# A retention / conformer / ConvFFN trunk step on one core: another order of the opening stage, one key split ahead of the gates, one product on VectorE, LayerNorm means in three PSUM banks

## The chip, the cores and the metric

One core of a Trainium2 chip runs the whole program; nothing else runs on the chip. The metric is the device time of one execution in microseconds, as a median over runs. The core has TensorE (PE, with its weight loads PEld), VectorE (DVE), ScalarE (ACT), GpSimd (POOL) and the queue engine SyncE (SP), all synchronised by semaphores written out by hand in the kernel.

## The reference, cut to what matters

One layer (DEPTH = 1) is applied to 1024 latent tokens and, apart from them, to 128 context tokens, all in float32:

```python
mod = silu(cond) @ ada_w + ada_b              # cond = c (latent) or c_ctx (context); 6 x 1024 columns
sh1, sc1, g1, sh2, sc2, g2 = split(mod, 6)
h    = rms_norm(x, n1_pre) * (1 + sc1) + sh1
proj = h @ w_in                               # 8192 columns: q, k, v, g | u_a, u_b | gate_ret, gate_conv
o, s_f, s_b = bidirectional_retention(rope(q), rope(k), v, ...)   # chunks of 128, 4 heads of 256
ret  = (silu(g) * head_group_norm(o)) @ ret_w_out
u    = depthwise_conv31(u_a * sigmoid(u_b))
conv = silu(layer_norm(u, cln_w, cln_b)) @ conv_w_out
x    = x + g1 * rms_norm((sigmoid(gate_ret) * ret + sigmoid(gate_conv) * conv) @ w_mix_out, n1_post)
h2   = rms_norm(x, n2_pre) * (1 + sc2) + sh2
a, b = split(depthwise_conv3(h2 @ ffn_w_up), 2)       # 2 x 2816 columns
x    = x + g2 * rms_norm((silu(a) * b) @ ffn_w_down, n2_post)
```

The outputs are x of both parts and the final states s_f, s_b of the context tokens.

## The kernel before, in words

**Arithmetic.** Every large matmul is made of three with 32-bit reduced operands: each factor is split into a high part (`*_hi`, a rounded copy, mostly on ScalarE) and a low part (`*_lo` = value minus high, on GpSimd or VectorE), and hi x hi, hi x lo and lo x hi are summed in PSUM (line 936 is the helper `mm` for nearly all of them). The 1152 tokens are 9 tiles of 128 (`NT`), or 3 groups of 384 (`NTG`, `TG`); 1024 features are 8 blocks `k` (`KT`). Each engine runs one program in written order; what sets the order is the code alone, and each piece waits for counts of semaphores.

**Opening.** Columns 0 to 2047 of `ada_w` (8 chunks `ada_p` of 1 MB, `ada_early`) are multiplied by silu(cond) as each lands. x comes in three loads (`x_load`, tiles 0-2, 3-5, 6-7, and the context tile). ScalarE squares x (`square`, `root`), VectorE scales it (`normed`). `mod_turns` turns the rows of mod into columns. Then 24 units j = 8 g + k (group g, block k) go through a chain: TensorE turns three tiles of x (`x_turn`, banks 5, 7, 6), ScalarE applies shift and scale (`modulated`, result `hf`), VectorE splits into `A_hi`, `A_lo` (`halves`; for some units, `ON_ACT`, ScalarE writes `A_hi` too). `first_u` multiplies them by the first two 128-column pieces of w_in: per group g the piece e = 0, block by block as the chain delivers, and then e = 1. `first_u` is followed by `q_half(0)`, whose first bank is free when ScalarE has read the result of e = 0 (`sig`, line 1500). The weight pieces come through four raw slots (`chunk_load`, SyncE), `split_w` (ScalarE) and `lo_w` (GpSimd).

**Projections** (96 to 727 us of the profile): TensorE runs without a gap; VectorE does rotary products and the 31-tap convolution, ending with the last channel block.

**Retention** (from 727 us): steps s = -9 to 35. In a step TensorE does, for the key/value chunk `piece(s)`, the outer product `outer_b` (needs `kb_lo` of GpSimd and `vb_lo` of VectorE, each after ScalarE's `key_b`), and between the parts of the recurrence a third of a gate projection (`gate_part(x)`, 24 matmuls, x = 0 to 47). `W_GATE0` gates stand ahead of the steps; the table `gate_of` gives the others to steps. The key/value chunks come back from memory in three slots (`kv_load`).

**Merge.** 16 tiles `n` of three groups (e = 3 n + g). The LayerNorm of the convolution branch runs beside the first tiles: GpSimd sums over blocks (`ln_tree`), TensorE averages over partitions by a matmul with `mean_w` (`ln_mean` after e = 5, 6, 8, `ln_var` after e = 11, 13, 15), VectorE centres (`c_raw`, line 2437).

**ConvFFN.** 22 column pairs j. The first two (`plain`) are multiplied directly, the others by seven products of sums (operands `O_hi`, `O_lo`; units A11, S2, S3, A22, S1, A12, S4), with token sums `T_raw`, `T_hi`, `T_lo` built on VectorE at the beginning. Per j: `centre_tap` (ScalarE, `f_cv`), `side_taps` (VectorE), `silu`, `product` (the SwiGLU product, in place in `f_cv[0]`), and `g_store` to memory, after which `centre_tap(j + 1, 0)` may overwrite `f_cv[0]`:

```python
if j and kind == 0:
    act.wait_ge(q.g_st, 16 * j)
```

## Time and profile before

| | us |
|---|---|
| median of 3 runs (2215.16 to 2217.37) | 2216.73 |
| the profiled execution | 2214.35 |
| its span | 2212.4 |
| TensorE busy | 2147.2 (97%) |
| VectorE busy | 1580.7 (71%) |
| ScalarE busy | 787.5 (36%) |
| GpSimd busy | 975.2 (44%) |

The profile page divides one execution by engine, by time and by group of instructions. TensorE's busy share is high nearly everywhere; of its 40 slices of 55 us only the first (7 tenths) and second (8 tenths with the weight loads) stand out. Therefore the rows that matter are those in which TensorE waits, and those of the engines that end its waits. A matmul's busy time is modelled; its start, and the distance between starts, are measured.

### The profile page before, as it was taken

The numbers are of one execution on the slowest core, as the hardware profiler recorded it, in microseconds if no ns is written. First come the engines' busy times: TensorE is split into PE (matmuls) and PEld (weight loads), VectorE is DVE, ScalarE is ACT, GpSimd is POOL, SyncE is SP. The second block draws the span as 40 slices with busy tenths as digits, with TensorE's granted clock in tenths as the row PEclk, the third lists the DMA queues.
The fourth block names the chain that finished last, engine by engine and source line by source line (L and its number), as shares of the span: only waits on it lengthen the run. The fifth ranks groups of instructions, "written<-read, shape, count | busy, mean of one in ns | idle before, by whom it ended". The sixth has DMA issues, their size and how long they took to land.

```text
span 2212.4 us, 31598 instructions
## 1 busy us (share of the span) xinstructions
PE 2147.2 (97%) x12483; PEld 1968.5 (89%) x12483; DVE 1580.7 (71%) x1789; ACT 787.5 (36%) x1328; POOL 975.2 (44%) x620
## 2 busy tenths in 40 slices
PE   7899999999999899999999999989999999999998
PEld 3788988988988799999889998889999999978887
DVE  3489589589589467676436536689998898766775
ACT  3501201101101266665537333343333333434342
POOL 0313423423323356665372230056665665565654
PEclk9999999999999999999999999999999999999999
DMA  9333342442432445545454444313232322385653
GB/s 304 105 119 102 120 126 92 129 128 86 130 105 87 151 149 169 165 147 156 158 193 156 131 163 137 105 30 84 66 89 61 82 68 74 116 298 172 210 176 130
DMA packets 246578, 291.78 MB, mean 132 GB/s; under 512 B 12225, under 2 KB 198945, under 8 KB 246433
## 3 DMA queue, kind: packets, MB, share of 16 engines
q1 hardware_dynamic: 175553, 219.22, 31.3%
q10 hardware_dynamic: 69472, 65.83, 9.2%
q0 software_dynamic: 1408, 4.72, 0.5%
...
## 4 chain that ended last, share of the span: by engine, by line
PE 88%; DVE 4%; DMA 2%; ACT 2%; POOL 1%; issue 1%; SPq 0%; ACTq 0%; DVEq 0%; POOLq 0%
PE ps L936 87%; DVE f_cv L2550 1%; DMA ada_p<-in_ada_w 1%; POOL f_cv L2099 1%; PE ps L1146 1%; DVE T_raw L2510 1%; PE ps L1194 0%; DMA r_raw<-rT_d 0%; PE ps L987 0%; DMA sh_row<-gain_d 0%; DVE T_lo L2532 0%; DMA g_raw<-g_d 0%; ACT f_cv L1842 0%; PE ps L1281 0%; POOL Wa_lo L1955 0%
## 5 line engine op out<-in xcount | busy, mean ns | idle before, releaser
L2230 DVE SCALAR_TENSOR_TENSOR conv_y<-u_in,VC,conv_y 128x1167 f32<-128x1167 f32 x240 | 396.0, 1650 | 7.4
L1955 POOL TENSOR_TENSOR Wa_lo<-W_raw,Wa_hi 128x1024 fp32r<-128x1024 f32 x58 | 142.7, 2467 | 409.4 <-ACT Wa_hi L1404 409.3
L936 PE MATMUL ps<-A_hi,Wa_hi 128*128 128x384 f32 x768 | 270.8, 353 | 6.2 <-DVE A_lo L2195 5.3
L936 PE MATMUL ps<-A_hi,Wa_lo 128*128 128x384 f32 x768 | 258.9, 337 | 0.0
L936 PE MATMUL ps<-A_lo,Wa_hi 128*128 128x384 f32 x768 | 258.7, 337 | 0.0
L2550 DVE SCALAR_TENSOR_TENSOR f_cv<-f_in,VF,f_cv 128x1023 f32<-128x1023 f32 (+1 forms) x176 | 210.7, 1248 | 11.2 <-ACT f_cv L1842 9.4
L1955 POOL TENSOR_TENSOR D_lo<-F_raw,D_hi 128x1024 fp32r<-128x1024 f32 x66 | 162.4, 2463 | 99.6 <-ACT D_hi L1404 99.6
L2587 DVE TENSOR_TENSOR g_lo<-g_raw,g_hi 128x384 fp32r<-128x384 f32 x66 | 138.6, 2110 | 81.1 <-ACT g_hi L1404 81.1
L2094 POOL TENSOR_TENSOR O_lo<-E,O_hi 128x512 fp32r<-128x512 f32 x80 | 130.4, 1630 | 147.1 <-ACT O_hi L1404 147.1
L936 PE MATMUL ps<-Wb_hi,A_hi 128*128 128x512 f32 x432 | 180.0, 417 | 0.0
L936 PE MATMUL ps<-Wb_hi,A_lo 128*128 128x512 f32 x432 | 170.7, 395 | 0.0
L2094 POOL TENSOR_TENSOR O_lo<-F_raw,O_hi 128x512 fp32r<-128x512 f32 x68 | 111.5, 1642 | 132.2 <-ACT O_hi L1404 132.2
L936 PE MATMUL ps<-Wb_lo,A_hi 128*128 128x512 f32 x432 | 169.3, 392 | 0.0
L936 PE MATMUL ps<-D_hi,g_hi 128*128 128x512 f32 x396 | 155.2, 392 | 4.4 <-POOL D_lo L1955 2.4
L936 PE MATMUL ps<-D_hi,g_lo 128*128 128x512 f32 x396 | 154.6, 390 | 0.0
L936 PE MATMUL ps<-D_lo,g_hi 128*128 128x512 f32 x396 | 154.6, 390 | 0.0
L936 PEld LDWEIGHTS ps<-A_hi,Wa_hi 128*128 128x128 f32 x768 | 145.7, 190 | 9.6 <-DVE A_lo L2195 5.6
L1404 ACT ACTIVATE Wa_hi<-W_raw 128x1024 fp32r<-128x1024 f32 x58 | 60.4, 1056 | 255.7 <-DVE qk_st L2256 211.0
L936 PE MATMUL ps<-B_hi,O_hi 128*128 128x288 f32 x608 | 141.6, 297 | 5.5 <-POOL O_lo L2094 4.9
L936 PEld LDWEIGHTS ps<-A_lo,Wa_hi 128*128 128x128 f32 x768 | 145.7, 190 | 0.8
L936 PEld LDWEIGHTS ps<-A_hi,Wa_lo 128*128 128x128 f32 x768 | 145.0, 189 | 0.0
L936 PE MATMUL ps<-B_hi,O_lo 128*128 128x288 f32 x608 | 141.2, 297 | 0.0
...
## 6 DMA issues: line engine op xcount, KB each, us to landing
...
```

The source lines that it names most:

```text
L936: return pe.matmul(out, l, r, start=start, stop=stop)
L1146: last = pe.transpose(ps[:, 2, x * P:(x + 1) * P], qt[:, n % 5, x // 2, (x % 2) * P:(x % 2 + 1) * P], ident[:, :])
L1404: return act.activation(dst, src, ACT.Copy)
L1955: return pool.tensor_tensor(dst, x, Fv(hi), ALU.subtract)
L2094: pool.tensor_tensor(O_lo[o % 4][:, :, :], op_src(o)[2], Fv(O_hi[o % 4][:, :, :]), ALU.subtract).then_inc(q.w_lo, 1)
L2099: pool.tensor_tensor(f_cv[0][:, :], f_cv[0][:, :], f_cv[1][:, :], ALU.mult).then_inc(q.fprod, 1)
L2230: dve.scalar_tensor_tensor(out=y, in0=x, scalar=tap, in1=y, op0=ALU.mult, op1=ALU.add).then_inc(q.conv_step, 1)
L2510: dve.tensor_tensor(out, x, y, op).then_inc(q.t_ok, 1)
L2550: dve.scalar_tensor_tensor(out=f_cv[kind][:, o[0]:o[1]], in0=f_in[kind][:, x[0]:x[1]], scalar=VF[:, col:col + 1], in1=f_cv[kind][:, o[0]:o ...
L2587: dve.tensor_tensor(g_lo[c % 4][:, :], g_raw[c % 4][:, :], Fv(g_hi[c % 4][:, :]), ALU.subtract).then_inc(q.dg_lo, 1)
```

## The change

The change has five parts.

1. **Transfers of the opening.** The two condition vectors go first on SyncE's queue and have a semaphore of their own (`c_in`); the first transpose waits for them alone. Four semaphores instead of two let chunk n of `ada_w` be issued when chunk n - 4 has landed. The second load of x is issued behind chunk 7, and with the third load and the raw pieces 2 to 5 behind it. The first loads of `ada_w`'s later columns, the rotary tables and the norm weights move from ScalarE's queue to SyncE's.
2. **Order of the opening on the engines.** `x_turn` stands ahead of the block's matmuls and not behind; ScalarE's second squares come behind the first weight split, its third squares after unit 7 (before: after unit 11); VectorE scales the second tiles of x at unit 3 and the third at unit 8 (before: ahead of all units, and at unit 12); `ON_ACT` holds for units 1, 4, 7, 9, 12, 15; weight pieces 1 to 5 are split after units 3, 15, 19, 21, 23.
3. **Retention.** `key_b(0)` on ScalarE and GpSimd and `value_b(0)` on VectorE come ahead of the gates and of VectorE's mod columns; one gate instead of two stands ahead of the steps, and step -9 gets a gate.
4. **LayerNorm.** The three means are written to banks 4, 5, 6 and the three variances to 7, 4, 5, so that `ln_mean(g)` no longer waits for `centre` of g - 1.
5. **ConvFFN.** `product(0)` moves from GpSimd to VectorE, behind `side_taps(0, 1)`.

```diff
-        ada_in = [q.ada_in0, q.ada_in1]
+        ada_in = [q.ada_in0, q.ada_in1, q.ada_in2, q.ada_in3]
...
-        W_GATE0, N_STEP = 2, HEADS * NT
+        W_GATE0, N_STEP = 1, HEADS * NT
         gate_of, n_gate = {}, W_GATE0
-        for s_ in [-8, -7, -6, -5, -4, -2, -1] + list(range(N_STEP)):
+        for s_ in [-9, -8, -7, -6, -5, -4, -2, -1] + list(range(N_STEP)):
...
-        ON_ACT = lambda k: k % 4 == 3
+        ON_ACT = lambda j: j < 2 * KT and j % KT % 3 == 1
...
+        LN_BANK = {("mean", 0): 4, ("mean", 1): 5, ("mean", 2): 6, ("square", 0): 7, ("square", 1): 4, ("square", 2): 5}
...
             def ada_chunk(n):
 
-                if n >= 2:
-                    sp.wait_ge(ada_in[n % 2], 16 * (n // 2))
-                sp.dma_start(ada_p[:, n, :, :], ada[:, :, n * 2 * P:(n + 1) * 2 * P]).then_inc(ada_in[n % 2], 16)
+                if n >= 4:
+                    sp.wait_ge(ada_in[n % 4], 16)
+                sp.dma_start(ada_p[:, n, :, :], ada[:, :, n * 2 * P:(n + 1) * 2 * P]).then_inc(ada_in[n % 4], 16)
...
+            sp.wait_ge(q.hT_lo, N_A)
+            for x in range(2):
+                sp.dma_start(ada_w[:, x, :, :], ada[:, :, (16 + x) * P:(17 + x) * P]).then_inc(ada_in[x], 16)
...
             pe.wait_ge(q.ident_ok, 3)
-            pe.wait_ge(q.tab_in, 80)
+            pe.wait_ge(q.c_in, 32)
...
             for n in range(8):
-                if n == 3:
+                if n == 4:
                     row_turns()
...
                         for k in range(KT):
+                            ahead = KT * g + (k + 4 if e == 0 else 11 + (k // 2 if g else 0))
+                            while turned < min(ahead, N_A):
+                                x_turn(turned)
+                                turned += 1
                             if e == 0:
                                 pe.wait_ge(q.hT_lo, KT * g + k + 1)
                             mm(o, wh[:, k, :], A_hi[:, tiles, k, :], k == 0, False)
                             mm(o, wh[:, k, :], A_lo[:, tiles, k, :], False, False)
                             last = mm(o, wl[:, k, :], A_hi[:, tiles, k, :], False, k == KT - 1)
-                            ahead = KT * g + (k + 4 if e == 0 else 11 + k // 2)
-                            while turned < min(ahead, N_A):
-                                x_turn(turned)
-                                turned += 1
...
             def ln_mean(g):
 
                 pe.wait_ge(q.ln_sum, 3 * LN_SUM_MEAN[g])
-                if g:
-                    pe.wait_ge(q.ln_dve, ln_done["centre", g - 1])
                 tok = slice(g * TG, (g + 1) * TG)
-                mm(ps[:, 6, 0:TG], mean_w[:, :], c_sq[:, 0, tok], True, True).then_inc(q.ln_pe, 1)
+                mm(ps[:, LN_BANK["mean", g], 0:TG], mean_w[:, :], c_sq[:, 0, tok], True, True).then_inc(q.ln_pe, 1)
...
-            for g in range(2):
+            def squares(g):
+
                 for t in range(3 * g, 3 * g + 3):
                     square(t)
                 root(g)
+            squares(0)
             split_w(0)
-            split_w(1)
+            squares(1)
             act.wait_ge(q.mod_ok, 2)
             for j in range(N_A):
                 modulated(j)
-                if j == 11:
-                    for t in range(6, NT):
-                        square(t)
-                    root(2)
-                if j in (15, 19):
-                    split_w((j - 15) // 4 + 2)
+                if j == 7:
+                    squares(2)
+                if j in (3, 15, 19, 21, 23):
+                    split_w((3, 15, 19, 21, 23).index(j) + 1)
...
-            act.wait_ge(q.hT_lo, N_A)
-            ada_load(0)
-            ada_load(1)
-            for r in range(3):
-                rope_load(r)
-            gn_load(0)
-            gn_load(1)
...
+            key_b(0)
             for x in range(W_GATE0):
                 gate_out(x)
                 if x == 0:
                     split_w(N_S1 + 2, (q.q_ps, 72))
-            key_b(0)
...
             for o in range(2 * 4):
                 op_lo(o)
-            product(0)
             for x in (U_A11, U_S2, U_S3, U_A22):
                 op_lo(op_no(2, x))
...
+            meaned(0)
             normed(0)
             row_half(0)
...
             row_half(1)
+            meaned(1)
             dve.wait_ge(q.ada_used, 16)
...
             for j in range(N_A):
-                if j == 12:
+                if j == 3:
+                    normed(1)
+                if j == 8:
+                    meaned(2)
                     normed(2)
                 halves(j)
...
             side_taps(0, 1)
+            dve.wait_ge(q.ftap, max(tap_no(0, 0), tap_no(0, 1)))
+            dve.wait_ge(q.fsilu, 1)
+            dve.tensor_tensor(f_cv[0][:, :], f_cv[0][:, :], f_cv[1][:, :], ALU.mult).then_inc(q.fprod, 1)
             T_lo_part(0)
```

What that makes of the order, at three places. SyncE's queue from the program's start, before (`rows` are the small parameter vectors, `ada_p` the chunks of 1 MB, x3 and x4 are that many transfers):

```order
L643 DMA ada_p<-in_ada_w 128x8x256 x2
L638 DMA x_all<-in_x_sample 128x3x1024
...
L643 DMA ada_p<-in_ada_w 128x8x256 x4
L638 DMA x_all<-in_x_sample 128x3x1024
L643 DMA ada_p<-in_ada_w 128x8x256 x2
L697 DMA W_raw<-in_w_in 128x8x128 x2
L638 DMA x_all<-in_x_sample 128x2x1024
```

and the same queue now:

```order
L650 DMA rows<-in_c 8x128
L650 DMA rows<-in_c_ctx 8x128
L647 DMA ada_p<-in_ada_w 128x8x256 x2
L642 DMA x_all<-in_x_sample 128x3x1024
L647 DMA ada_p<-in_ada_w 128x8x256 x2
...
L647 DMA ada_p<-in_ada_w 128x8x256 x3
L701 DMA W_raw<-in_w_in 128x8x128
L647 DMA ada_p<-in_ada_w 128x8x256
L642 DMA x_all<-in_x_sample 128x3x1024
L701 DMA W_raw<-in_w_in 128x8x128
```

Two more chunks stand ahead of the small vectors (the line of dots), and the second load of x stands behind the last chunk.

ScalarE at the beginning of retention, before (from the last mod columns; `gate_sg` is a gate's read-out, `kb_hi` and `vb_hi` the key and value split, `st_b` the state's output):

```order
L1404 ACTIVATE mod<-ps 128x16
L1404 ACTIVATE gate_sg<-ps 128x384
L1577 DMA gate_d<-gate_sg 128x384
L1404 ACTIVATE Wa_hi<-W_raw 128x1024
L1404 ACTIVATE gate_sg<-ps 128x384
L1577 DMA gate_d<-gate_sg 128x384
L1404 ACTIVATE kb_hi<-kv 128x256
L1587 ACTIVATE vb_hi<-kv,dkt 128x256
L1404 ACTIVATE st_b<-ps 128x512
```

and now:

```order
L1419 ACTIVATE mod<-ps 128x16
L1419 ACTIVATE kb_hi<-kv 128x256
L1592 ACTIVATE vb_hi<-kv,dkt 128x256
L1419 ACTIVATE gate_sg<-ps 128x384
L1582 DMA gate_d<-gate_sg 128x384
L1419 ACTIVATE Wa_hi<-W_raw 128x1024
L1419 ACTIVATE st_b<-ps 128x512
L1663 DMA out<-st_b 128x2x256
L1419 ACTIVATE kb_hi<-kv 128x256
L1592 ACTIVATE vb_hi<-kv,dkt 128x256
L1419 ACTIVATE gate_sg<-ps 128x384
```

The first split moved ahead of both read-outs, and the second split stands ahead of the second read-out.

GpSimd in the same place, before and then now (`conv_d` is the store of the last convolution block, two transfers):

```order
L1997 TENSOR_TENSOR vg_st<-vg_st,gn_head 128x256 x9
L1955 TENSOR_TENSOR Wa_lo<-W_raw,Wa_hi 128x1024
L1976 DMA conv_d<-conv_y 128x1024
L1976 DMA conv_d<-conv_y 128x128
L1955 TENSOR_TENSOR kb_lo<-kv,kb_hi 128x256 x3
```

```order
L2002 TENSOR_TENSOR vg_st<-vg_st,gn_head 128x256 x9
L1960 TENSOR_TENSOR kb_lo<-kv,kb_hi 128x256
L1960 TENSOR_TENSOR Wa_lo<-W_raw,Wa_hi 128x1024
L1981 DMA conv_d<-conv_y 128x1024
L1981 DMA conv_d<-conv_y 128x128
L1960 TENSOR_TENSOR kb_lo<-kv,kb_hi 128x256 x2
```

Only the first `kb_lo` moved; the weight split and the store are still ahead of the second.

## Rows read from the trace of the kernel before

**Rows 1.** waits of TensorE, whole program: us in total, times, longest

```profile
PE ps L936 <- POOL O_lo L2094: 4.9, 2, 4.4
...
PE ps L936 <- DVE c_raw L2437: 4.1, 1, 4.1
```

**Rows 2.** timeline of TensorE, opening: start, us, line, what, count [idle before]

```profile
10.88 0.25 PE L952 MATMUL ps<-ident,rows 16*128 16x16 f32 x1 [10.88 <-DMA dec<-in_ret_decay_bwd]
...
11.65 13.34 PE L936 MATMUL ps<-ada_p,cs 128*2 128x256 f32 x48 [0.52 <-ACT cs L1421]
...
42.55 3.61 PE L936 MATMUL ps<-ada_p,cs 128*2 128x256 f32 x16
...
70.23 0.45 PE L936 MATMUL ps<-A_hi,Wa_hi 128*128 128x384 f32 x1 [2.56 <-DVE A_lo L2195]
...
95.72 0.80 PE L936 MATMUL ps<-Wa_hi,A_hi 128*128 128x512 f32 x1 [5.30 <-ACT sig L1500]
```

**Rows 3.** timeline of SyncE's queue, opening

```profile
9.36 15.16 SPq L643 DMA_DIRECT2D ada_p<-in_ada_w  x4
```

**Rows 4.** tile ada_p, from issue to landing

```profile
DMA to landing us min/median/max: 5.3/10.1/13.2
```

**Rows 5.** stretch 30 to 40 us: its us, engines busy, TensorE's clock, DMA, GB/s

```profile
30.00:40.00 10.00, 8.44 (x41) 3.15 (x39) 2.83 (x6) 3.43 (x7) 0.00 (x0) 1.00 1.08 357
```

**Rows 6.** timeline of ScalarE, opening

```profile
34.00 1.06 ACT L1438 ACTIVATE sq_t<-x_all 128x1024 f32<-128x1024 f32 x1 [7.08 <-DMA x_all<-in_x_sample]
...
48.60 1.79 ACT L1455 ACTIVATE hf<-ps,mod,hscale 128x384 f32<-128x384 f32 x3 [3.33 <-DVE hscale L2208]
```

**Rows 7.** timeline of VectorE, opening

```profile
50.95 0.56 DVE L2195 TENSOR_TENSOR A_lo<-hf,A_hi 128x384 fp32r<-128x384 f32 x1
...
67.05 2.08 DVE L2181 TENSOR_SCALAR x_all<-x_all,rst 128x1024 f32<-128x1024 f32 x3
...
75.00 1.47 DVE L2195 TENSOR_TENSOR A_lo<-hf,A_hi 128x384 fp32r<-128x384 f32 x1
```

**Rows 8.** timeline of GpSimd, opening

```profile
73.66 2.40 POOL L1955 TENSOR_TENSOR Wa_lo<-W_raw,Wa_hi 128x1024 fp32r<-128x1024 f32 x1 [25.41 <-ACT Wa_hi L1404]
```

**Rows 9.** timeline of TensorE, start of retention

```profile
738.67 0.35 PE L936 MATMUL ps<-vb_hi,kb_hi 128*128 128x256 f32 x1 [2.60 <-DVE vb_lo L2286]
...
742.42 0.55 PE L936 MATMUL ps<-vb_hi,kb_hi 128*128 128x256 f32 x1 [2.80 <-DVE vb_lo L2286]
...
755.40 0.38 PE L936 MATMUL ps<-vb_hi,kb_hi 128*128 128x256 f32 x1 [0.49 <-POOL kb_lo L1955]
```

**Rows 10.** timeline of SyncE's queue, start of retention

```profile
742.96 3.07 SPq L719 DMA_DIRECT2D kv<-qkvg_d  x3
```

**Rows 11.** tile kv, 720 to 745 us, from issue to landing

```profile
DMA to landing us min/median/max: 8.5/8.6/8.7
```

**Rows 12.** stretches in which TensorE's granted clock was 0.5

```profile
92.50:99.30 6.80, 3.58 (x9) 2.92 (x10) 0.00 (x0) 6.05 (x6) 6.80 (x3) 0.50 0.53 169
...
1133.60:1136.90 3.30, 3.14 (x8) 2.56 (x9) 0.02 (x1) 2.76 (x1) 0.95 (x2) 0.50 0.02 5
...
1474.90:1478.20 3.30, 3.30 (x16) 3.30 (x15) 0.25 (x1) 1.63 (x2) 0.00 (x0) 0.50 1.07 273
```

**Rows 13.** timeline of GpSimd, start of ConvFFN

```profile
1461.22 11.60 POOL L2099 TENSOR_TENSOR f_cv<-f_cv,f_cv 128x1152 f32<-128x1152 f32 x1 [12.13 <-DVE f_cv L2550]
```

**Rows 14.** timeline of ScalarE, start of ConvFFN

```profile
1476.57 1.35 ACT L1842 ACTIVATE f_cv<-f_in,VF 128x1152 f32<-128x1152 f32 x1 [16.17 <-DMA g_d<-f_cv]
```

**Rows 15.** timeline of VectorE, start of ConvFFN

```profile
1439.36 1.36 DVE L2510 TENSOR_TENSOR T_raw<-T_raw,T_raw 128x1152 f32<-128x1152 f32 x1
...
1467.81 2.55 DVE L2510 TENSOR_TENSOR T_raw<-T_raw,B_lo 128x2304 f32<-128x2304 f32 x1
...
1477.95 4.01 DVE L2550 SCALAR_TENSOR_TENSOR f_cv<-f_in,VF,f_cv 128x1023 f32<-128x1023 f32 x4 [7.60 <-ACT f_cv L1842]
...
1494.53 2.47 DVE L2583 TENSOR_TENSOR f_in<-ps,f_in 128x576 f32<-128x576 f32 x3
```

More of the change, by code:

```diff
@@ L495, in s_no @@
             return 4 * (j - PLAIN) + which
-        wl_base = [sum(32 if m < N_S1 and m % 6 >= 2 else 16 for m in range(N_L) if chunk_sem(m) == x) for x in range(4)]
+        wm_base = [sum(32 if m < N_S1 and m % 6 >= 2 else 16 for m in range(N_L) if chunk_sem(m) == x) for x in range(4)]
+        wl_base = [wm_base[x] + (16 * M_CHUNKS // 3 if x < 3 else 0) for x in range(4)]
         tile_base = [16 * len(range(x, HEADS * NT, 5)) for x in range(5)]
@@ L639, in ada_chunk @@
             def ada_chunk(n):
-                if n >= 2:
-                    sp.wait_ge(ada_in[n % 2], 16 * (n // 2))
-                sp.dma_start(ada_p[:, n, :, :], ada[:, :, n * 2 * P:(n + 1) * 2 * P]).then_inc(ada_in[n % 2], 16)
+                if n >= 4:
+                    sp.wait_ge(ada_in[n % 4], 16)
+                sp.dma_start(ada_p[:, n, :, :], ada[:, :, n * 2 * P:(n + 1) * 2 * P]).then_inc(ada_in[n % 4], 16)
+            for n, name in enumerate(("c", "c_ctx")):
+                v = a[name] if len(a[name].shape) == 1 else a[name][0]
+                sp.dma_start(rows[n * KT:(n + 1) * KT, 0, :], v.rearrange("(k p) -> k p", p=P)).then_inc(q.c_in, 16)
             ada_chunk(0)
@@ L702, in chunk_load @@
                                      w_in_s[:, 2 * j:2 * j + 2, 2 * g + s, h * 256:(h + 1) * 256]).then_inc(done, 16)
-            for n in range(2):
-                chunk_load(n)
+            for n in range(4, 7):
+                ada_chunk(n)
+            chunk_load(0)
+            ada_chunk(7)
+            x_load(1)
+            chunk_load(1)
             sp.wait_ge(x_in[0], X_IN[0])
@@ L1411, in split_w @@
                 copy(w_hi[chunk_slot(n)], chunk_raw(n)).then_inc(q.w_hi, 1)
-            for n, name in enumerate(("c", "c_ctx")):
-                v = a[name] if len(a[name].shape) == 1 else a[name][0]
-                act.dma_start(rows[n * KT:(n + 1) * KT, 0, :], v.rearrange("(k p) -> k p", p=P)).then_inc(q.tab_in, 16)
             act.dma_start(tab[:, :], a["shape_table"]).then_inc(q.tab_in, 16)
@@ L1451, in modulated @@
                 outs = [t3(hf[:, j % 6, :])]
-                if ON_ACT(k):
+                if ON_ACT(j):
                     outs.append(A_hi[:, 3 * g:3 * g + 3, k, :])
@@ L2192, in halves @@
                 hi, lo = (x[:, 3 * g:3 * g + 3, k, :] for x in (A_hi, A_lo))
-                if not ON_ACT(k):
+                if not ON_ACT(j):
                     then(dve.tensor_copy(hi, h_))
@@ L2265, in _, with value_b @@
                     taps_u(i, range(2 * NT, CW))
+            def value_b(b):
+                dve.wait_ge(q.kb_hi_ok, 2 * b + 2)
+                dve.scalar_tensor_tensor(out=vb_lo[:, :], in0=kv[:, b % 3, 1, :], scalar=dkt[:, b // 8, 3:4], in1=Fv(vb_hi[:, :]),
+                                         op0=ALU.mult, op1=ALU.subtract).then_inc(q.kb_vlo, 1)
+            value_b(0)
             dve.wait_ge(q.adaU_ok, 4)
```

82 lines of the change are left out of this document (42 added, 40 removed).

## The prediction

> **What bounds the kernel now.** I read the page's table of engines and the slices first: TensorE works in 97% of the span, and only the first two of its 40 slices stand out. So I listed TensorE's waits and looked which of them the change touches. Four places came out.
>
> - Opening. TensorE does nothing until 10.88, when the last small table lands; its first transpose waits for all five [rows 2]. Three chunks of `ada_w` then take 13.34 and later ones 3.61 each, so at full clock the three would be 10.8. Chunk 7 ends at 42.55 + 3.61 = 46.16, ScalarE's first `modulated` starts at 48.60 [rows 6], and the chain's 24 units set the time from there: `first_u` ends at 95.72 - 5.30 = 90.42. Behind it stands one wait of 5.30 for `sig`, and from 92.5 to 99.3 the granted clock is 0.50 (1.2 of 2.4 GHz) after that idle time [rows 12].
> - Retention: two waits of 2.60 and 2.80 for `vb_lo`, with matmuls of 0.55 after them where 0.35 is usual [rows 9].
> - LayerNorm: one wait of 4.1 for `c_raw` [rows 1], and a clock of 0.50 from 1133.6 to 1136.9 [rows 12].
> - ConvFFN: a wait of 4.4 for `O_lo` [rows 1] and half clock at 1474.9 to 1478.2 with DMA share 1.07 [rows 12]. Behind it lies a GpSimd product of 11.60 [rows 13], a `centre_tap` that waited 16.17 for the product's store [rows 14], and VectorE, idle 7.60 ahead of the side taps [rows 15].
>
> In the projections, from 95.72 to retention, TensorE runs without a gap, so what the opening gains arrives at the end in full.
>
> **The opening, up to the first unit.** The condition vectors now go first and alone release the transpose. An `ada_p` load needs at least 5.3 from issue to landing [rows 4]; TensorE can start chunk 0 near 8 in place of 11.65. Chunk 0 at half clock is 7.2 and chunk 1 is 3.6, so chunk 2 starts near 19 (before: 25.0 - 3.6 = 21.4). Six chunks are 6 x 3.61 = 21.7, and I allow 1.5 for the two sets of turns between them: chunk 7 ends at 42.2. The distance from there to the first unit was 48.60 - 46.16 = 2.4 and I keep it: first unit at about 45.0, **-3.6**. Supply: eight chunks and the first x are 10.0 MB, at 357 GB/s [rows 5] 28 us after the start, so chunk 7 is there by 34 while TensorE wants it at 38.6. The second x, now behind chunk 7, has 2.1 MB more in front (with the first raw weight): issue by 31, landing by 36 to 41, since each of SyncE's issues can hold the queue (four took 15.16 [rows 3]). Its squares need three times 1.06 [rows 6], to about 44.3. The bounds are 0 (x late, then ScalarE comes late) and -6 (chunk 0 starts at 7 with nothing lost).
>
> **The 24 units.** Before, 48.60 to 90.42: 41.8. Removed is part of the wait of 2.56 at the group's change [rows 2], because the third squares come four units earlier, -1.1; TensorE's transposes stand one block earlier, and `ON_ACT` takes A_hi for different units, -2.4. Added is that five weight splits instead of two run on GpSimd while VectorE splits. One such split is 2.40 on GpSimd [rows 8], and a VectorE instruction beside it took 1.47 instead of 0.56 [rows 7]: 0.9 each for three more, 2.7, of which two thirds lie in VectorE's idle time, +0.9. The scaling of the second x (2.08 for three [rows 7]) stands between units 2 and 3 instead of before them and is hidden by the time in which ScalarE is ahead: 0 to +2. Sum **-2.6**, bounds -6 and +5.
>
> **The hand-over to `q_half(0)`.** The wait of 5.30 arose since splits, twelve loads on ScalarE's own queue and a table load stood between the last unit and `sig`. The loads are gone from there and the weights are split earlier, so `sig` comes with the end of the e = 0 part: **-5.3** (bounds -3 and -5.3), and with no gap the stretch at half clock goes. In its 6.8 us the first 3.6 after 95.72 were work at half speed: **-1.8** (0 to -1.8). `ada_w`'s next load now waits for the last unit; its user stands near 84 and the load needs up to 13.2 [rows 4] in the worst case; I put 0 for it, at most +0.5 of TensorE beside the other q pieces. Opening together: -3.6 - 2.6 - 5.3 - 1.8 = **-13.3**; bounds -6 and -18.
>
> **Retention.** The first key split comes before the gates, so the wait of 2.60 goes. The second does not go whole: on GpSimd the weight split (2.40, by the like in the opening [rows 8]) and the store still stand ahead of `kb_lo(1)`, which leaves about 1.4 of 2.80. Without these waits the steps come earlier, and chunk 3 now meets its own load. It is issued at 742.96 [rows 10] behind a wait for the convolution's store, lands 8.5 later [rows 11] = 751.5, and with the splits the outer product starts at 753.1 at best, against 755.40 before [rows 9]. So at most 2.3 can be gained by then, and about 1.6 comes back as a longer idle time with the clock at half behind it: **-0.7** (bounds +1 and -6; the latter if the load too is issued earlier).
>
> **LayerNorm.** `ln_mean(1)` waited 4.1 for VectorE to have centred group 0, in the same bank. With banks of its own it needs GpSimd's sum alone, which no row shows late. So the 4.1 goes, and half of the 3.3 at half clock: **-5.7** (bounds 0, if GpSimd's sum is late in its place, and -5.8).
>
> **ConvFFN.** A VectorE product of that shape takes 1.36 [rows 15], in place of 11.60. VectorE runs on, without idle time, until 1470.36 (1467.81 + 2.55); with the product ahead of this the side taps of j = 1 can start at 1470.36 + 1.4 = 1471.8, not at 1477.95: 6.1 earlier. The product is done by 1462.6 and its store had time; `centre_tap(1, 0)` needs 1.35 [rows 14] and is done by 1471. The chain onwards (VectorE's sums at 1494.53 [rows 15], which hold TensorE) moves by the same amount, less what TensorE's own work limits. GpSimd, rid of the product, splits `O_lo` when it is due, and the 4.4 and most of the half clock behind it go. VectorE's 1.4 moves `T_lo` later by as much: **-5.5** (bounds -1.6 and -7.6).
>
> The Trainium skill ("SBUF — State Buffer", section "Who interferes with whom") says that VectorE and GpSimd share a port pair that is an exclusive lock: where both instructions need it, and one with two SBUF inputs does, the second to issue waits until the first is done. The product's 11.60 [rows 13] is in keeping with that; the 1.47 against 0.56 [rows 7] beside a split of 2.40 [rows 8] is not the full length of the split. By that rule the ConvFFN term would be at its full bound, and the splits in the opening would be a rival, below.
>
> **The sum.** -13.3 - 0.7 - 5.7 - 5.5 = -25.2; the profiled execution's own 2214.35 gives 2189.2. The median is 2.4 above that execution, so on its scale 2191.6, and I say **2192**.
>
> **The rivals.**
> - *The second x holds ScalarE.* The queue lets x go only once chunk 7 is issued; if it lands near 45 and not 41, its squares, which stand ahead of the first unit, end at 48.4, and the first unit starts where it did. For: an issue takes 3.8 us on this queue [rows 3], and DMA is full in that stretch (1.08 [rows 5]). Against: with four semaphores the chunks themselves wait less. -25.2 + 3.6 + 1.4 more for the group phase = -20.2: 2197. Chance 0.20.
> - *GpSimd blocks VectorE for the whole split.* Five splits lie among the units now; if each stops VectorE for 2.4 and not 0.9, that is 5 x 1.5 = 7.5 more: -17.7, 2199. For: 11.60 for one product beside an unbroken VectorE. Against: 1.47 beside 2.40. This is the page's rule of the exclusive lock. Chance 0.10.
> - *Everything counts in full.* The kv load is early, both `vb_lo` waits go with their half clock (-5), ConvFFN at -7.6: -32, 2185. Chance 0.10.
> - *The opening stays at half clock: slower.* TensorE now begins earlier than the data flow, and has a pause before every chunk. If therefore 1.2 GHz is granted through the opening, each of six chunks takes 7.2 instead of 3.6 (+21.6) and the 144 matmuls of `first_u`, 384 columns each, 0.32 instead of 0.16 (+23): together about +45 on a base of -25 + 13 (the opening's other gains become meaningless as TensorE bounds it) gives +10 to +33, middle about 2230. It decides only if over half of 8 to 85 us is at 1.2 GHz. For: 48 matmuls from 11.65 show a slow start, and idle stretches of 4 to 5 us are followed by half clock [rows 12]. Against: 1.00 in 30 to 40 us with TensorE busy 8.44 of 10 [rows 5]. Chance 0.03.
> - The forecast: 0.57.
>
> **How the numbers follow.** The likeliest case alone has 2186 to 2199 (opening -18 to -8, the others' bounds partly cancelling). With the two rivals above it and the one below, 2183 to 2204 leaves out under 2 in 10. A change of under 0.2% (4.4 us) can hardly be told from none; only a loss of most terms brings it there. Faster 0.95, same 0.02, slower 0.03.
>
> **What would show it.** TensorE's first matmul near 5 and chunk 7 ending near 42; the first `modulated` near 45; `q_half(0)`'s start near 83 with no wait for `sig`, and a clock of 1.00 behind it. VectorE's `A_lo` at 1.5 beside each split, not 2.9. In retention no wait of 2.60, and a new one, for the load of the key/value chunk or its splits, at the fourth outer product. No wait for `c_raw`. A product of 1.4 on VectorE, and the side taps of j = 1 about 10 us after it and not 16.8 us after GpSimd's start. I am wrong if `modulated` starts at 48 (first rival), if `A_lo` takes over 2 us (second), or if ln's matmul waits as long for GpSimd as it did for VectorE.

## The result, and the profile after

The changed kernel takes 2197.05 us in the median (2195.45 to 2200.72), before 2217.05; the ratio is 0.9914 (95% interval 0.9899 to 0.9929). That is 20.0 us faster where 25 were forecast (2192), inside the stated range. The profiled execution took 2197.59, its span 2195.8 against 2212.4. So the profiled pair is 16.8 apart and the medians are 20.0 apart: the kernel before was profiled in an execution 2.7 under its median, the changed one 0.5 over.

The sum came nearer than its terms, as the table shows. Its last column comes from laying the two traces over each other, matmul by matmul ("the overlay" from here on): how much earlier each one starts.

| part | forecast | overlay, profiled pair |
|---|---|---|
| opening, read at 100 us and still so at 728 | -13.3 | -4.8 |
| retention, read at 1100 us | -0.7 | -3.7 (-2.6 by 800 us) |
| LayerNorm | -5.7 | -6.0 at 1200 us, of which 1.1 is lost again by 1440 |
| ConvFFN, 1440 to 1600 us | -5.5 | -4.0 |
| sum | -25.2 | -17.4 (last matmul -17.0, spans -16.6) |

The recorded expectations below give other figures for the same four parts: 4.5, 3.8, 5.2 and 3.9. The table's are read at the places that it names.

TensorE's waits over the whole program (us in total, times, longest), for [rows 1]. First one more of the kernel before:

```profile
PE ps L936 <- DVE A_lo L2195: 5.3, 5, 2.6
```

and then those of the changed kernel:

```profile
PE ps L953 <- DVE A_lo L2198: 7.3, 6, 2.6
PE ps L953 <- DMA ada_p<-in_ada_w: 7.0, 2, 6.2
...
PE ps L953 <- POOL kb_lo L1960: 4.9, 3, 2.9
PE ps L953 <- ACT f_in L1419: 4.0, 1, 4.0
PE ps L969 <- DMA rows<-in_c_ctx: 3.9, 1, 3.9
...
PE ps L953 <- POOL O_lo L2099: 0.9, 2, 0.5
```

The waits for `c_raw` and `sig` are gone and the longest for `O_lo` is 0.5, as forecast. But the waits for `A_lo` have risen from 5.3 to 7.3, and in place of the 4.4 for `O_lo` stand 4.0 for `f_in`. TensorE's timeline of the opening and of the first outer products, for [rows 2, 9]:

```profile
3.93 0.26 PE L969 MATMUL ps<-ident,rows 16*128 16x16 f32 x1 [3.93 <-DMA rows<-in_c_ctx]
10.42 8.98 PE L953 MATMUL ps<-ada_p,cs 128*2 128x256 f32 x32 [6.23 <-DMA ada_p<-in_ada_w]
20.20 7.17 PE L953 MATMUL ps<-ada_p,cs 128*2 128x256 f32 x32 [0.80 <-DMA ada_p<-in_ada_w]
...
39.77 3.62 PE L953 MATMUL ps<-ada_p,cs 128*2 128x256 f32 x16
...
54.77 0.44 PE L953 MATMUL ps<-A_hi,Wa_hi 128*128 128x384 f32 x1 [2.63 <-DVE A_lo L2198]
...
86.56 0.69 PE L953 MATMUL ps<-A_hi,Wa_hi 128*128 128x384 f32 x1 [1.96 <-DVE A_lo L2198]
...
92.66 0.39 PE L953 MATMUL ps<-Wa_hi,A_hi 128*128 128x512 f32 x1
...
726.92 0.28 PE L953 MATMUL ps<-vb_hi,kb_hi 128*128 128x256 f32 x1
...
733.49 0.39 PE L953 MATMUL ps<-vb_hi,kb_hi 128*128 128x256 f32 x1 [1.51 <-POOL kb_lo L1960]
...
746.43 0.35 PE L953 MATMUL ps<-vb_hi,kb_hi 128*128 128x256 f32 x1 [2.90 <-POOL kb_lo L1960]
```

TensorE is ready at 4 and then waits 6.2 us for chunk 0. Chunk 7 ends at 43.39 (before 46.16), and ScalarE's first unit starts at 45.81, 2.8 earlier. From there to `q_half(0)` it is 46.9 us. Before, `first_u` ended 41.8 after the first unit; the forecast had 39.2. In retention the wait of 2.60 is gone, the second is 1.51 where about 1.4 was forecast, and the forecast new wait at the fourth outer product is there (2.90).

The first rival asked whether the late second x holds ScalarE:

```profile
41.87 1.06 ACT L1450 ACTIVATE sq_t<-x_all 128x1024 f32<-128x1024 f32 x1 [5.77 <-DMA x_all<-in_x_sample]
```

It landed at 41.9 (forecast 36 to 41, the rival near 45), and its squares end at 45.1, just before the first unit. So it came later than forecast, but it did not put the first unit at 48.

VectorE in the units, for [rows 7]:

```profile
49.48 4.19 DVE L2184 TENSOR_SCALAR x_all<-x_all,rst 128x1024 f32<-128x1024 f32 x3
...
72.14 1.45 DVE L2198 TENSOR_TENSOR A_lo<-hf,A_hi 128x384 fp32r<-128x384 f32 x1
...
75.14 2.71 DVE L2198 TENSOR_TENSOR A_lo<-hf,A_hi 128x384 fp32r<-128x384 f32 x1
...
78.35 2.23 DVE L2198 TENSOR_TENSOR A_lo<-hf,A_hi 128x384 fp32r<-128x384 f32 x1
...
84.24 2.26 DVE L2198 TENSOR_TENSOR A_lo<-hf,A_hi 128x384 fp32r<-128x384 f32 x1
```

and GpSimd beside it, for [rows 8]:

```profile
49.76 2.69 POOL L1960 TENSOR_TENSOR Wa_lo<-W_raw,Wa_hi 128x1024 fp32r<-128x1024 f32 x1 [11.23 <-ACT Wa_hi L1419]
70.79 2.38 POOL L1960 TENSOR_TENSOR Wa_lo<-W_raw,Wa_hi 128x1024 fp32r<-128x1024 f32 x1 [18.34 <-ACT Wa_hi L1419]
75.04 2.40 POOL L1960 TENSOR_TENSOR Wb_lo<-W_raw,Wb_hi 128x1024 fp32r<-128x1024 f32 x1 [1.87 <-ACT Wb_hi L1419]
77.80 2.36 POOL L1960 TENSOR_TENSOR Wb_lo<-W_raw,Wb_hi 128x1024 fp32r<-128x1024 f32 x1 [0.36 <-ACT Wb_hi L1419]
83.73 2.36 POOL L1960 TENSOR_TENSOR Wb_lo<-W_raw,Wb_hi 128x1024 fp32r<-128x1024 f32 x1 [3.57 <-ACT Wb_hi L1419]
```

Add start and duration in both lists. The last four splits end at 73.17, 77.44, 80.16, 86.09; the four `A_lo` end at 73.59, 77.85, 80.58, 86.50, each 0.41 or 0.42 later. Alone an `A_lo` takes 0.56. So it waits for the whole rest of the split and then does its work.

The Trainium skill ("SBUF — State Buffer", section "Who interferes with whom") says just this: whichever of the two issues first keeps the shared port pair for its whole instruction, and the other is blocked until then. The four ends above agree. It could be read from the rows of before as well: 73.66 + 2.40 = 76.06 and 75.00 + 1.47 = 76.47 [rows 7, 8], again 0.41. The prediction took this 1.47 as evidence against the rule; it is what the rule gives when `A_lo` comes late in the split.

TensorE's clock, in stretches (its us, engines busy, clock, DMA share, GB/s), for [rows 12]:

```profile
48.50:51.90 3.40, 3.40 (x16) 3.16 (x13) 3.33 (x5) 2.87 (x5) 2.14 (x1) 0.50 0.59 186
55.30:58.70 3.40, 3.40 (x15) 3.11 (x14) 2.49 (x5) 2.34 (x5) 0.00 (x0) 0.50 0.01 5
86.00:89.40 3.40, 2.85 (x9) 2.85 (x10) 0.50 (x1) 1.13 (x1) 2.18 (x2) 0.50 0.48 133
1461.70:1468.30 6.60, 4.67 (x19) 4.70 (x20) 6.60 (x6) 4.92 (x8) 3.87 (x1) 0.50 0.01 2
```

Three such stretches lie between the first unit and `q_half(0)`. Before, one of that length lay there (from 51.5), and one of 6.8 began in the wait for `sig` [rows 12]; none follows `q_half(0)` now, as forecast.

ConvFFN, VectorE, for [rows 15]:

```profile
1448.86 1.36 DVE L2614 TENSOR_TENSOR f_cv<-f_cv,f_cv 128x1152 f32<-128x1152 f32 x1
...
1456.88 3.65 DVE L2523 TENSOR_TENSOR T_raw<-T_raw,B_lo 128x2304 f32<-128x2304 f32 x1
1460.45 2.99 DVE L2563 SCALAR_TENSOR_TENSOR f_cv<-f_in,VF,f_cv 128x1023 f32<-128x1023 f32 x4
```

and ScalarE, for [rows 14]:

```profile
1453.91 1.35 ACT L1847 ACTIVATE f_cv<-f_in,VF 128x1152 f32<-128x1152 f32 x1 [6.89 <-DMA g_d<-f_cv]
...
1460.57 2.12 ACT L1419 ACTIVATE T_hi<-T_raw 128x2304 fp32r<-128x2304 f32 x1 [4.78 <-DVE T_raw L2523]
1462.60 1.23 ACT L1419 ACTIVATE f_in<-ps 128x576 f32<-128x576 f32 x3
```

The product takes 1.36 and the side taps start 11.6 after it began, near the 10 forecast. But the last `T_raw` took 3.65, not 2.55, and ends at 1460.53. When it started, GpSimd was in a low part:

```profile
1455.86 2.26 POOL L2099 TENSOR_TENSOR O_lo<-E,O_hi 128x512 fp32r<-128x512 f32 x1 [9.83 <-ACT O_hi L1419]
```

The fourth `T_hi` waits for `T_raw`, and behind that in ScalarE's order stand the evictions of `f_in` (its copies out of PSUM), on which TensorE waits 4.0.

### The profile page after: what moved, and what is told of

Same layout as the page of the kernel before. It is cut to its first block, busy times and chain, and to the rows that moved or that the text cites. A ratio compares the mean times of both kernels' runs of the same rounds, so it can differ in the third digit from the quotient of the medians.

```text
span 2195.8 us, 31594 instructions
## 1 busy us (share of the span) xinstructions
PE 2142.4 (98%) x12483; PEld 1965.5 (90%) x12483; DVE 1589.4 (72%) x1790; ACT 788.1 (36%) x1326; POOL 966.9 (44%) x619
## 4 chain that ended last, share of the span: by engine, by line
PE 90%; DVE 4%; DMA 2%; POOL 1%; ACT 1%; issue 1%; SPq 0%; ACTq 0%; DVEq 0%; POOLq 0%
PE ps L953 88%; DVE f_cv L2563 1%; DVE T_raw L2523 1%; PE ps L1163 1%; DMA ada_p<-in_ada_w 1%; DVE A_lo L2198 1%; POOL O_lo L2099 0%; DMA r_raw<-rT_d 0%; PE ps L1211 0%; DMA kv<-qkvg_d 0%; DMA sh_row<-gain_d 0%; DMA g_raw<-g_d 0%; DMA W_raw<-in_w_mix_out 0%; DVE A_hi L2197 0%; POOL f_cv L2104 0%
## 5 line engine op out<-in xcount | busy, mean ns | idle before, releaser
L2563 DVE SCALAR_TENSOR_TENSOR f_cv<-f_in,VF,f_cv 128x1023 f32<-128x1023 f32 (+1 forms) x176 | 216.1, 1279 | 3.8 <-ACT f_cv L1847 2.1
L953 PE MATMUL ps<-T_hi,O_hi 128*128 128x288 f32 x640 | 138.1, 298 | 4.5 <-ACT f_in L1419 4.0
```

Of the source, the lines that this page charges most:

```text
L953: return pe.matmul(out, l, r, start=start, stop=stop)
L2563: dve.scalar_tensor_tensor(out=f_cv[kind][:, o[0]:o[1]], in0=f_in[kind][:, x[0]:x[1]], scalar=VF[:, col:col + 1], in1=f_cv[kind][:, o[0]:o ...
```

## The experiments

All ratios are to the kernel before, run beside each kernel on the same chip. The two last columns are starts in us in the profiled execution.

| kernel | median (lowest to highest) | ratio (95%) | first unit | `q_half(0)` |
|---|---|---|---|---|
| before | 2217.05 (2215.16 to 2217.79) | | 48.60 | 95.72 |
| changed | 2197.05 (2195.45 to 2200.72) | 0.9914 (0.9899 to 0.9929) | 45.81 | 92.66 |
| rest_alone | 2203.86 (2201.95 to 2205.23) | 0.9941 (0.9925 to 0.9958) | 48.27 | 95.12 |
| undo_ret | 2199.91 (2198.67 to 2205.48) | 0.9929 (0.9915 to 0.9944) | 47.81 | 96.08 |
| undo_ln | 2203.37 (2203.27 to 2206.31) | 0.9943 (0.9929 to 0.9958) | 46.02 | 90.92 |
| undo_ffn | 2201.76 (2201.1 to 2202.57) | 0.9933 (0.9918 to 0.9948) | 46.89 | 93.94 |
| dve_lo | 2192.36 (2191.64 to 2193.34) | 0.9895 (0.988 to 0.9909) | 47.16 | 88.16 |
| hold1 | 2196.94 (2196.21 to 2199.45) | 0.9917 (0.9902 to 0.9932) | 46.12 | 94.14 |
| x1_early | 2198.78 (2197.73 to 2202.11) | 0.9926 (0.9911 to 0.9941) | 50.53 | 95.10 |
| x0_late | 2198.14 (2194.65 to 2200.78) | 0.9917 (0.99 to 0.9933) | 48.98 | 97.33 |
| act_order | 2197.84 (2192.99 to 2202.25) | 0.9913 (0.9896 to 0.9929) | 47.41 | 95.68 |
| norm_e1 | 2191.98 (2191.95 to 2193.19) | 0.9895 (0.988 to 0.991) | 46.89 | 87.26 |
| all_three | 2195.1 (2194.83 to 2195.21) | 0.9908 (0.9893 to 0.9922) | 47.26 | 87.58 |
| ops_first | 2190.65 (2190.32 to 2191.89) | 0.9887 (0.987 to 0.9903) | 45.58 | 85.91 |

The intervals of two kernels 3 us apart overlap, so such differences are argued from the traces.
The medians come from different chips: the kernel before had 2215.3 to 2215.8 beside the experiments and 2217.05 beside the changed kernel. A difference of 1 or 2 us between two medians therefore shows nothing by itself.

**The parts one by one.** The kernel before with the three later parts (3, 4 and 5) whole:

```diff
-        W_GATE0, N_STEP = 2, HEADS * NT
+        W_GATE0, N_STEP = 1, HEADS * NT
...
-                mm(ps[:, 6, 0:TG], mean_w[:, :], c_sq[:, 0, tok], True, True).then_inc(q.ln_pe, 1)
+                mm(ps[:, LN_BANK["mean", g], 0:TG], mean_w[:, :], c_sq[:, 0, tok], True, True).then_inc(q.ln_pe, 1)
...
-            product(0)
...
```

> The kernel before with the retention, LayerNorm and ConvFFN parts of the change, and with its own opening. The two traces, laid over each other matmul by matmul, give the opening 4.5 us, retention 3.8, LayerNorm 5.2 and ConvFFN 3.9. Theory (the parts add up, and the opening gave only a third of the 13.3 forecast): the span is 12.5 to 13.5 us under the 2212.4 of before, some 2204 in the median, and q_half(0) starts at 95.7 with the wait of 5.3 for sig as before. Rival (the parts lean on each other, the later ones gain only because the opening moved their loads): 6 to 10 us under before.

Measured: 11.9 under before in the median, 10.4 in the span. That lies between the theory (12.5 to 13.5) and the rival (6 to 10). The overlay on the kernel before is 0 from 100 us on, -0.2 at 800, -1.3 at 1100, -7.3 behind LayerNorm, -6.1 at 1440 and -10.2 behind ConvFFN's start. LayerNorm gave 6.0 and ConvFFN 4.1, as in the pair. Retention by 800 us gave only 0.2.

So the rival is right for retention. By 780 us it gave 1.0 to 2.8 in the four kernels that have it together with exactly the changed opening (the changed kernel, undo_ln, undo_ffn, act_order). The changed kernel is 6.8 under rest_alone in the medians and 7.2 in the overlay: 4.8 by the opening itself, 2.4 by retention behind it. The opening alone is 3.5 in the mean of five profiled executions (1.4 to 6.3).

Retention put back:

```diff
-        W_GATE0, N_STEP = 1, HEADS * NT
+        W_GATE0, N_STEP = 2, HEADS * NT
...
-            key_b(0)
             for x in range(W_GATE0):
                 gate_out(x)
                 if x == 0:
                     split_w(N_S1 + 2, (q.q_ps, 72))
+            key_b(0)
...
```

> The changed kernel with retention's beginning put back (key split 0 behind the gates, two gates ahead of the steps). My forecast for that part was 0.7 us of gain, held by a key/value load that would not move. Theory (the load is issued when TensorE's steps and the convolution's store let it, so it moves with them; the overlay gives 3.8): 3 to 5 us slower than the changed kernel, with waits of 2.6 and 2.8 for vb_lo back, and the fourth outer product about 4.5 us later relative to the waits ahead of it. Rival (my forecast: what is gained at the first two waits comes back at the fourth outer product): under 1.5 us slower.

The median is 2.9 above the changed kernel's. In the overlay on the changed kernel retention costs 2.6 by 800 us and 3.7 by 1100, and the waits of 2.60 and 2.78 are back. That is the theory. The rest is told by the key/value load ahead of the fourth outer product. SyncE's queue and ScalarE in the changed kernel:

```profile
737.65 1.47 SPq L736 DMA_DIRECT2D kv<-qkvg_d  x3
```

```profile
744.83 0.42 ACT L1419 ACTIVATE kb_hi<-kv 128x256 fp32r<-128x256 f32 x1 [4.15 <-DMA kv<-qkvg_d]
```

And in rest_alone, with the outer product:

```profile
742.42 2.02 SPq L720 DMA_DIRECT2D kv<-qkvg_d  x3
```

```profile
750.61 0.42 ACT L1403 ACTIVATE kb_hi<-kv 128x256 fp32r<-128x256 f32 x1 [5.13 <-DMA kv<-qkvg_d]
752.21 0.55 PE L937 MATMUL ps<-vb_hi,kb_hi 128*128 128x256 f32 x1 [3.84 <-POOL kb_lo L1954]
```

There issue and use are 8.2 apart, not 7.2, and the outer product starts at 752.21, where the prediction had 753.1 at best. Two stretches of half clock follow there (from 752.0 and 772.5), one in the changed kernel (from 765.3).

LayerNorm put back (the variances too are in one bank again, 7):

```diff
-                mm(ps[:, LN_BANK["mean", g], 0:TG], mean_w[:, :], c_sq[:, 0, tok], True, True).then_inc(q.ln_pe, 1)
...
                 if g:
                     pe.wait_ge(q.ln_dve, ln_done["centre", g - 1])
...
+                mm(ps[:, 6, 0:TG], mean_w[:, :], c_sq[:, 0, tok], True, True).then_inc(q.ln_pe, 1)
...
```

> The changed kernel with the means of the LayerNorm back in one bank, and so with the wait of the second mean for the first centring. Theory: the wait of 4.1 us for c_raw returns and with it a stretch of half clock of 3.4 us: 5 to 6 us slower than the changed kernel. Rival (GpSimd's sum would have ended the wait almost as late): under 2 us slower.

The median is 6.3 above the changed kernel's, and the wait is back to the tenth:

```profile
PE ps L952 <- DVE c_raw L2449: 4.1, 1, 4.1
```

The product put back on GpSimd (the two hunks of part 5 reversed):

```diff
             for o in range(2 * 4):
                 op_lo(o)
+            product(0)
...
-            dve.wait_ge(q.ftap, max(tap_no(0, 0), tap_no(0, 1)))
-            dve.wait_ge(q.fsilu, 1)
-            dve.tensor_tensor(f_cv[0][:, :], f_cv[0][:, :], f_cv[1][:, :], ALU.mult).then_inc(q.fprod, 1)
```

> The changed kernel with the first SwiGLU product back on GpSimd. My forecast for the part was 5.5 us, the overlay gives 3.9: a wait of 4.0 us for f_in stands in the changed kernel where none of that length was. Theory: 3 to 5 us slower than the changed kernel, with the product at 10 to 12 us on GpSimd again, the wait of 4 us for O_lo back and the one for f_in at 2.2. Rival (the product's place does not matter, the gain there came from the earlier parts): under 1 us slower.

The median is 4.7 above the changed kernel's. GpSimd's product is 11.60 again, and TensorE's longest wait for `O_lo` 4.4:

```profile
1448.74 11.60 POOL L2104 TENSOR_TENSOR f_cv<-f_cv,f_cv 128x1152 f32<-128x1152 f32 x1 [12.13 <-DVE f_cv L2564]
```

```profile
PE ps L953 <- POOL O_lo L2099: 5.8, 3, 4.4
```

**Why the units became slower.** The first four kernels are the changed one with one edit; the fifth, norm_e1, builds on the first. GpSimd's late splits given to VectorE, behind its last unit:

```diff
-            for n in range(6):
+            for n in range(2):
                 lo_w(n)
...
+                if i == 0:
+                    pool.wait_ge(q.w_lo, 6)
...
+            for n in range(2, 6):
+                dve.wait_ge(q.w_hi, n + 1)
+                if n == 2:
+                    dve.wait_ge(q.w_lo, 2)
+                dve.tensor_tensor(w_lo[chunk_slot(n)], chunk_raw(n), Fv(w_hi[chunk_slot(n)]), ALU.subtract).then_inc(q.w_lo, 1)
```

> The changed kernel, but the low parts of weight pieces 2 to 5 are made by VectorE behind its 24th unit, and not by GpSimd among the units. In the changed kernel VectorE's A_lo took 2.71, 2.23 and 2.26 us beside those splits, each ending 0.4 us after the split's end; first unit to q_half(0) was 46.9 us (first forecast: 39 to the end of first_u, before: 41.8). Theory (whichever of the two comes second waits until the other's instruction is done; five splits among the units cost that much): all A_lo of the third group 0.56, TensorE's waits of 1.6 and 2.0 there and the half clock near 86 gone, first unit to q_half(0) 42 to 44 us, 3 to 4 us faster than the changed kernel. Rival (the third group is bound by TensorE's turns or by ScalarE, the long A_lo are hidden): within 1 us of the changed kernel.

VectorE's timeline; the like `A_lo` took 2.71 and 2.26:

```profile
74.55 0.56 DVE L2200 TENSOR_TENSOR A_lo<-hf,A_hi 128x384 fp32r<-128x384 f32 x1
...
82.75 0.56 DVE L2200 TENSOR_TENSOR A_lo<-hf,A_hi 128x384 fp32r<-128x384 f32 x1
83.23 1.22 DVE L2231 TENSOR_TENSOR Wa_lo<-W_raw,Wa_hi 128x1024 fp32r<-128x1024 f32 x1
```

From the first unit to `q_half(0)` it is 41.0 us instead of 46.9. TensorE's waits for `A_lo` fell from 7.3 to 3.7 in all, and the half clock near 86 is gone. The kernel is 4.7 faster in the median, and its slowest run is faster than the changed kernel's fastest. In the overlay on the changed kernel 4.5 of this stands at 100 us already. The theory holds, and by more than it said.

GpSimd's piece 1 held back:

```diff
+                if n == 1:
+                    pool.wait_ge(q.xn_ok, 6)
```

> The changed kernel, but GpSimd's split of weight piece 1 waits until VectorE has scaled the second x. Side by side they took 2.69 and 4.19 us, where the scaling alone takes 2.08, and TensorE waited 2.63 behind them. Theory (half of that wait is the two engines stopping each other): the scaling takes 2.1, TensorE's wait there 0.5 to 1, and one half-clock stretch goes; 1 to 3 us faster than the changed kernel. Rival (the wait is the scaling's place among the units, and the split only moves its stop onto an A_lo): within 1 us.

```profile
49.78 2.08 DVE L2186 TENSOR_SCALAR x_all<-x_all,rst 128x1024 f32<-128x1024 f32 x3
...
52.36 2.81 DVE L2200 TENSOR_TENSOR A_lo<-hf,A_hi 128x384 fp32r<-128x384 f32 x2
```

The scaling is 2.08 again, but the two next `A_lo` take 2.81 (two took 1.03 in the changed kernel), and TensorE's longest wait is still 2.7. The median is the same. The rival holds: the stop only moves.

The second x early (with ScalarE's squares of it ahead of the first weight split, and its scaling ahead of the units):

```diff
+            x_load(1)
             for n in range(4, 7):
                 ada_chunk(n)
             chunk_load(0)
             ada_chunk(7)
-            x_load(1)
...
+            squares(1)
             split_w(0)
-            squares(1)
...
+            meaned(1)
+            normed(1)
             row_half(1)
-            meaned(1)
...
-                if j == 3:
-                    normed(1)
```

> The changed kernel, but the second load of x goes ahead of chunk 4 of ada_w, its squares ahead of the first weight split and its scaling ahead of the units. Theory (the late x costs by its scaling among the units, 4.2 us of VectorE and a TensorE wait of 2.6 with half clock behind): these go, the first unit stays at 45 to 47, and the kernel is 2 to 5 us faster than the changed one. Rival (supply is the limit: 1.6 MB more ahead of chunks 4 to 7 make TensorE wait for each of them): chunk 7 ends 2 to 4 us later and the kernel is no faster.

```profile
31.27 11.90 PE L953 MATMUL ps<-ada_p,cs 128*2 128x256 f32 x48 [4.51 <-DMA ada_p<-in_ada_w]
```

TensorE waits 4.5 for chunk 4, chunk 7 ends at 48.10 and the first unit comes at 50.53. The units take 44.6 us instead of 46.9, but more than that is lost ahead of them: the rival.

The first x late:

```diff
-            x_load(0)
             ada_chunk(2)
             ada_chunk(3)
+            x_load(0)
```

> The changed kernel, but the first load of x goes behind chunk 3 of ada_w and not behind chunk 1. TensorE waited 6.2 us for chunk 0, which landed 8.9 us after its issue beside other transfers; I had put its start at 8, it was 10.4. Theory (transfers issued together share the rate, so chunk 0 lands when all of them nearly do): chunk 0 is there by 8 to 9, chunk 7 ends 1.5 to 2 us earlier, but the first unit hardly moves, since the second x's squares end at 45.3: within 1 us of the changed kernel. Rival (chunk 0's landing is set by its own latency of 8 to 9 us): chunk 0 at 10.4 as before.

```profile
29.41 12.21 PE L953 MATMUL ps<-ada_p,cs 128*2 128x256 f32 x48 [2.18 <-DMA ada_p<-in_ada_w]
```

TensorE starts chunk 0 at 10.12 all the same, so it is not the bytes of x that hold it. That is the rival's number; whether it is the load's own latency or the chunks issued right behind it, no run separates. The first unit comes at 48.98, since chunk 4 is waited for as well (2.18).

The scaling moved to the two places between the groups, on top of dve_lo:

```diff
-                            ahead = KT * g + (k + 4 if e == 0 else 11 + (k // 2 if g else 0))
+                            ahead = KT * g + (min(k + 4, 8) if e == 0 else 8 if k < 4 else 11)
...
-                if j == 3:
+                if j == 8:
                     normed(1)
-                if j == 8:
+                if j == 10:
                     meaned(2)
+                if j == 16:
                     normed(2)
...
```

> As dve_lo (low parts of pieces 2 to 5 on VectorE), and VectorE scales the second x behind unit 7 and the third behind unit 15, while TensorE does the e = 1 part of the group ahead; TensorE's turns of the next group start in that part's second half. Theory (the scaling inside the units holds TensorE, whoever it shares with; in the e = 1 part TensorE has 4.2 us of work that needs nothing of VectorE): the waits of 2.6 for A_lo go, and two half-clock stretches near 50 and 57 go: 2 to 4 us faster than dve_lo, first unit to q_half(0) 38 to 39 us. Rival (the turns now come late, so the first A_lo of a group arrives behind the e = 1 part and a wait of the same size stands there): within 1 us of dve_lo.

```profile
PE ps L953 <- DVE A_lo L2203: 2.5, 7, 0.7
```

The longest wait for `A_lo` fell from 2.6 to 0.7, yet from the first unit to `q_half(0)` it is 40.4 against 41.0, and the median is 2191.98 against 2192.36. That is the rival's number, but not its mechanism, since no wait of the old size came back. Two half-clock stretches remain in the units, where the theory wanted them gone.

**ConvFFN's new wait.** On the changed kernel, the evictions ahead of the fourth `T_hi`:

```diff
-            T_hi_part(T_4)
             for n in range(3, 6):
                 evac(1, n)
+            T_hi_part(T_4)
```

> The changed kernel, but ScalarE reads out f_in (three evictions of column pair 1) ahead of the fourth T_hi and not behind it. In the changed kernel the fourth T_hi waited until 1460.57 for VectorE's last T_raw (ended 1460.53, lengthened from 2.55 to 3.65 and put 1.4 later by the product), the evictions came at 1462.6, and TensorE waited 4.0 us for f_in. Theory (the product's gain of 5.5 fell to 3.9 because T_raw, later on VectorE, now holds ScalarE and by it the evictions): the wait for f_in goes below 0.5, the half clock from 1461.6 to 1468.4 goes, the kernel is 3 to 5 us faster than the changed one. Rival (VectorE's side taps and token sums bound this place, so a wait for T_lo or for VectorE's additions takes its place): under 1.5 us faster.

```profile
PE ps L953 <- POOL O_lo L2099: 7.5, 2, 7.0
```

```profile
1467.69 6.21 POOL L2099 TENSOR_TENSOR O_lo<-E,O_hi 128x512 fp32r<-128x512 f32 x1 [5.17 <-ACT O_hi L1419]
```

The wait for `f_in` is gone and one of 7.0 for `O_lo` is there: GpSimd's low part, 1.3 alone, took 6.21 beside VectorE's back-to-back work. There is no gain in the median. The theory named rightly what held `f_in`, but not what its removal is worth; the rival had the size right, but the wait that took the place is another than the one it named.

The edits of norm_e1 and act_order together:

> norm_e1 and act_order together. Theory (opening and ConvFFN are apart, gains add up): the sum of what both give over the changed kernel, 2184 to 2189 us in the median if both theories hold, 2192 if only dve_lo's part is real.

The median is 2195.1, 3.1 above norm_e1, so the sum did not come. In ConvFFN a wait of 6.8 for `O_lo` stands in place of the 4.1 for `f_in`, as in act_order. But this is the smaller part: in the overlay on norm_e1 all_three is 2.7 later at 1440 us already, ahead of the edit (from 1084 us half clock lasts 6.8 us and not 3.4 there; why is open), and 3.3 later at the end.

Last, on norm_e1, the evictions and the two operands' high parts ahead of `T_hi`:

```diff
-            T_hi_part(T_4)
             for n in range(3, 6):
                 evac(1, n)
             op_hi(op_no(2, U_S3))
             op_hi(op_no(2, U_A22))
+            T_hi_part(T_4)
```

> norm_e1 with ScalarE's evictions of f_in and also the high parts of the next two operands (S3, A22) ahead of the fourth T_hi. With the evictions alone moved (all_three), the wait for f_in of 4.1 us became one of 6.8 for O_lo: GpSimd began that low part at 1460.21, beside VectorE's unbroken run, and took 6.21 for what is 1.3 alone. Theory (the low part must start before VectorE's T_lo and side taps stand back to back; begun 3 to 4 us earlier it gets through): the wait for O_lo stays under 2 us, 3 to 5 us faster than norm_e1, 2187 to 2189 in the median. Rival (wherever it starts in VectorE's run, GpSimd gets through only in a gap of VectorE): a wait of 4 to 7 us for O_lo, no faster than norm_e1 (2192) and up to 3 us slower.

```profile
PE ps L953 <- DVE T_lo L2556: 4.4, 1, 4.4
```

The longest wait for `O_lo` is 0.5, as the theory said. But now TensorE waits 4.4 for `T_lo`: beside GpSimd's low parts VectorE's side taps take 6.10 for four (2.99 in norm_e1) and two `T_lo` 6.09 (5.02). The median of 2190.65 is 1.3 under norm_e1, less than the theory's 3 to 5; the wait that the rival wanted did not come. It is the fastest kernel here, 6.4 under the changed one, and its slowest run is faster than the changed kernel's fastest.

## Why the prediction was right, and where it was not

- **The opening up to the first unit** (-3.6): -2.8 in the profiled pair, -0.8 to -2.8 over the five kernels with exactly this opening. The start of chunk 0 was put at 8 and was 10.4, that of chunk 2 at 19 and was 20.2. The loads have little room here: TensorE waits 6.2 for chunk 0 and 0.8 for chunk 2, and x1_early and x0_late, which shift 1.6 MB among the chunks, let it wait 4.5 and 2.2 for chunk 4 too.
- **The 24 units** (-2.6): the step that failed. From the first unit to `q_half(0)` it was 46.9, and thus the units took 5.1 more than before instead of 2.6 less, 7.7 more than forecast. I took 0.9 for a stop from a row in which VectorE met only the end of a split, put two thirds of three such stops into idle time, and held normed(1) to be hidden. The stop is the whole rest of the other's instruction: 0.9, 2.15, 1.7 and 1.7 in the four `A_lo`, and 2.1 in the scaling (4.19 instead of 2.08). dve_lo shows it, by 5.9 us. The second rival (2199) had this mechanism and its 7.5 us, and its sign, `A_lo` over 2 us, is met three times; I gave it 0.10. The result, 2197.05, lies nearer to it than to the 2192 of the forecast.
- **The hand-over** (-5.3, -1.8): the wait for `sig` is gone, and the clock behind `q_half(0)` is full, as said. Another stretch of half clock, at 86.0, lies ahead of it, in the units.
- **Retention** (-0.7): the mechanism was right with the old opening and mis-sized with the new one. In rest_alone the load is issued at 742.42 (forecast 742.96), the outer product starts at 752.21 (forecast 753.1 at best), and 0.2 is left by 800 us. In the changed kernel it is 2.6 by then and 3.7 by 1100. The forecast took the load as fixed against a program that starts earlier; it moved along. That the distance from issue to use is 1.0 shorter with the new opening, and half clock there costs 1.4 less, was not explained by any run.
- **LayerNorm** (-5.7): 6.0 in the pair and in rest_alone (of which 1.1 and 1.2 are lost again by 1440), +6.3 when undone. Right.
- **ConvFFN** (-5.5): 3.9 to 4.1. The product and the side taps came as said. What was left out is what stands ahead of `T_raw` on VectorE: 1.4 of product and 1.1 of stop beside GpSimd, which ScalarE's order passes on to `f_in`. The sentence "1.4 moves `T_lo` later" named the wrong follower.

So the total inside the range owes something to luck. The opening, over half of the forecast, gave 4.8 of 13.3. Retention gave 3.0 more than forecast, the medians are 3 us further apart than the profiled pair, and the range was 21 us wide.
